# A four-layer diffusion backbone on one core: split activations stored half by half with a gap, weight slots moved by 0, 64, 320 and 384 bytes

## The reference, cut to what matters

```python
h = x * (1 + scale) + shift
x = layer_norm(alpha * x + gate * f(h))        # once with f = mixer, once with f = conv_ffn
def conv_ffn(h, w_up, conv_w, conv_b, w_down):
    u = dwconv_centred(h @ w_up, conv_w, conv_b)      # 1024 -> 2 * 2816
    gate, val = jnp.split(u, 2, axis=-1)
    return (jax.nn.silu(gate) * val) @ w_down         # 2816 -> 1024
```

## Time and profile before

| | before |
|---|---|
| median of the runs | 2409.9 us (2 runs, 2409.35 to 2410.45) |
| profiled execution, first to last instruction | 2413.2 us |
| PE busy | 2340.2 us, 97% |
| DVE, ACT, POOL busy | 70%, 47%, 14% |
| TensorE's granted clock, mean | 0.991 |
| chain that ended last, share on L1690 | 74% |

### The profile page before, as it was taken

How to read it: one execution, slowest core, us unless ns; L and a number is a source line. 1 busy time by engine, 2 the same in 40 slices (tenths; PEclk the granted TensorE clock), 3 DMA queues, 4 the chain that set the end, 5 groups by cost and what they waited for, 6 DMA issues and landing times.

```text
span 2413.2 us, 35782 instructions
## 1 busy us (share of the span) xinstructions
PE 2340.2 (97%) x13872; PEld 1903.1 (79%) x13872; DVE 1696.3 (70%) x2583; ACT 1129.2 (47%) x1948; POOL 335.6 (14%) x269
## 2 busy tenths in 40 slices
PE   6999999999999989999999999899999999989998
PEld 3765888888888559888879877788888889848998
DVE  3376689988444777999875236768999845487875
ACT  3466643442442576434324444455434325386663
POOL 0000311111110003111112003422111102002110
PEclk9999999999999999999999999999999999999999
DMA  8621645557233113555563421043555645404664
GB/s 260 204 71 39 215 142 164 166 148 208 81 97 92 30 58 100 166 157 166 162 180 86 113 70 45 2 132 114 166 163 158 192 116 125 129 13 123 187 180 132
DMA packets 449420, 310.94 MB, mean 129 GB/s; under 512 B 11922, under 2 KB 404674, under 8 KB 448996
## 3 DMA queue, kind: packets, MB, share of 16 engines
q1 hardware_dynamic: 446480, 307.09, 43.2%
q10 hardware_dynamic: 2772, 1.56, 0.2%
HBM read 307.56 MB, written 1.05 MB: 128 GB/s over the span
## 4 chain that ended last, share of the span: by engine, by line
PE 85%; DVE 6%; ACT 4%; issue 2%; DMA 2%; ACTq 0%; SPq 0%; DVEq 0%
PE bank L1690 74%; PE bank L1973 2%; DMA slab_raw<-in_mod_w 2%; PE bank L1993 1%; PE bank L2037 1%; ACT p L793 1%; DVE slab_lo L1047 1%; DVE stat L1316 1%; ACT hb L610 1%; DVE q_part L1375 1%; PE bank L1749 1%; PE bank L1768 1%; ACT slab_hi L595 1%; ACT pt L805 1%; PE bank L2165 1%
## 5 line engine op out<-in xcount | busy, mean ns | idle before, releaser
L1690 PE MATMUL bank<-h_hi,slab_hi 128*128 128x512 f32 (+1 forms) x2416 | 841.9, 348 | 4.1 <-DVE h_lo L1112 2.5
L1690 PE MATMUL bank<-h_hi,slab_lo 128*128 128x512 f32 (+1 forms) x2416 | 828.9, 343 | 0.0
L1690 PE MATMUL bank<-h_lo,slab_hi 128*128 128x512 f32 (+1 forms) x2416 | 828.9, 343 | 0.0
L1047 DVE TENSOR_TENSOR slab_lo<-slab_raw,slab_hi 128x1024 fp32r<-128x1024 f32 (+1 forms) x388 | 526.2, 1357 | 296.1 <-ACT slab_hi L595 294.8
L595 ACT ACTIVATE slab_hi<-slab_raw 128x1024 fp32r<-128x1024 f32 (+1 forms) x388 | 400.8, 1034 | 303.8 <-PE bank L1690 228.0
L1690 PEld LDWEIGHTS bank<-h_hi,slab_hi 128*128 128x128 f32 x2416 | 458.0, 190 | 85.6 <-issue 19.8
L1690 PEld LDWEIGHTS bank<-h_hi,slab_lo 128*128 128x128 f32 x2416 | 458.0, 190 | 53.8
L1690 PEld LDWEIGHTS bank<-h_lo,slab_hi 128*128 128x128 f32 x2416 | 458.3, 190 | 53.3 <-issue 0.5
L1021 ACT ACTIVATE conv<-bank,prm 128x512 f32<-128x512 f32 (+1 forms) x176 | 127.7, 725 | 446.6 <-PE bank L1690 446.6
L1072 DVE SCALAR_TENSOR_TENSOR mod_sum<-slab_raw,cond_wide,mod_sum 128x512 f32<-128x512 f32 x420 | 316.5, 812 | 0.3 <-DMA slab_raw<-in_mod_w 0.2
L1690 PE MATMUL bank<-g_hi,slab_hi 128*128 128x512 f32 (+1 forms) x788 | 272.0, 345 | 0.0
(11 more groups left out here) (248 smaller groups left out, 2658.0 us busy)
## 6 DMA issues: line engine op xcount, KB each, us to landing
slab_raw<-in_ffn_w_up SPq DMA_DIRECT2D x176, 512.0 KB, 3.9
slab_raw<-in_mod_w SPq DMA_DIRECT2D x168, 512.0 KB, 4.6
slab_raw<-in_ffn_w_down SPq DMA_DIRECT2D x64, 512.0 KB, 3.6
slab_gap<-in_mod_w SPq DMA_DIRECT2D x24, 512.0 KB, 7.6
slab_raw<-in_ffn_w_down SPq DMA_DIRECT2D x32, 384.0 KB, 3.2
slab_raw<-in_b_w_qkv SPq DMA_DIRECT2D x24, 512.0 KB, 3.8
slab_raw<-in_c_w_in SPq DMA_DIRECT2D x24, 512.0 KB, 3.8
slab_raw<-in_d_w_qkv SPq DMA_DIRECT2D x24, 512.0 KB, 3.8
```

The source lines that it names most:

```text
L1047: nc.vector.tensor_tensor(wlo[slot][:, 0:w], raw[of][:, 0:w], whi[slot][:, 0:w].bitcast(f32), ALU.subtract).then_inc(s_lo, 1)
L1690: ins = mm(out, l, r, start=first and n == 0, stop=last and n == 2, skip_group_check=parted)
```

## The change

1. `h_hi` and `h_lo` become `[P, 2, DT * CTX + H_GAP]`: first the context tokens of all 8 feature tiles (8192 bytes), then a gap of 80 float32 (320 bytes), then the latents of all 8 tiles. `g_hi` and `g_lo` become `[P, 2, FT * CTX + G_GAP]` with `G_GAP = 0`. A whole product is now one matmul with a moving access pattern of two rows of 256; a half has one row.
2. Slot s of the weights starts `SLOT_STEPS[s]` = 0, 64, 320 or 384 bytes (modulo 512) behind `h_hi`, and `whi[s]` and `wlo[s]` of a slot lie next to each other.
3. Small tensors (`coef0`, `coef1`, `small`) move into the gaps and `state[1][1]` behind `spread`; nothing else moves in time.
4. All accesses go through new views; PSUM banks and work tiles are viewed as two rows of 256 where the other operand is.

The distances, modulo 512 bytes, of moving operand less loaded weights in the same slot:

| slot | h, first half (context) | h, second half (latents) | g, either half |
|---|---|---|---|
| before, all | 0 | 0 | 64 |
| 0 | 0 | 320 | 448 |
| 1 | 448 | 256 | 384 |
| 2 | 192 | 0 | 128 |
| 3 | 128 | 448 | 64 |

A whole product of `h` has the first number while its first 256 columns move and the second after them. (For `g`: the tensors between are now 4736 + 4096 + 768 + 64 + 2048 + 1152 = 12864 = 25 x 512 + 64 bytes, behind slot 3's 384, which makes 448 behind `h_hi`.)

```diff
+SLOT_STEPS = (0, 64, 320, 384)
+H_GAP, G_GAP = 80, 0
...
-        h_hi, h_lo = place("h_hi", [P, DT, T], f32r), place("h_lo", [P, DT, T], f32r)
+        h_hi = place("h_hi", [P, 2, DT * CTX + H_GAP], f32r)
+        top[0] -= 8 * H_GAP % 512
+        h_pads = [[top[0] - 4 * H_GAP + 8 * H_GAP % 512], [top[0] + 4 * DT * CTX]]
+        h_lo = place("h_lo", [P, 2, DT * CTX + H_GAP], f32r)
+        top[0] -= 4 * H_GAP
         raw = [place(f"slab_raw{s}", [P, SLAB]) for s in range(SLOTS)]
-        whi = [place(f"slab_hi{s}", [P, SLAB], f32r) for s in range(SLOTS)]
-        wlo = [place(f"slab_lo{s}", [P, SLAB], f32r) for s in range(SLOTS)]
+        whi, wlo = [], []
+        for s in range(SLOTS):
+            top[0] += (h_at[0] + SLOT_STEPS[s] - top[0]) % 512
+            whi.append(place(f"slab_hi{s}", [P, SLAB], f32r))
+            wlo.append(place(f"slab_lo{s}", [P, SLAB], f32r))
...
-        g_hi, g_lo = place("g_hi", [P, FT, T], f32r, at=at), place("g_lo", [P, FT, T], f32r, at=at)
+        g_hi, g_lo = (place(n, [P, 2, FT * CTX + G_GAP], f32r, at=at) for n in ("g_hi", "g_lo"))
...
+        def tiles_of(x, k, c):
+            first, last = c.start // CTX, (c.stop - 1) // CTX
+            if first != last:
+                return x[:, :, CTX * k:CTX * k + CTX]
+            start = CTX * k + c.start - CTX * first
+            return x[:, first, start:start + c.stop - c.start]
+        def like(x, c):
+            return x[:, c].rearrange("p (s t) -> p s t", t=CTX) if c.stop - c.start == T else x[:, c]
...
-                nc.scalar.activation(h_hi[:, 2 * pr:2 * pr + 2, c], hb[b][:], ACT.Copy).then_inc(s_hhi, 1)
+                nc.scalar.activation(pair_of(h_hi, pr, c), hb[b][:], ACT.Copy).then_inc(s_hhi, 1)
...
-                    nc.scalar.activation(g_hi[:, j, c], g32[j % 2][:, c], ACT.Copy).then_inc(s_ghi, 1)
+                    nc.scalar.activation(tiles_of(g_hi, j, c), like(g32[j % 2], c), ACT.Copy).then_inc(s_ghi, 1)
...
-                    ins = three(out[:, c], whi[slot][:, wc], wlo[slot][:, wc], x_hi[:, k0 + k, c], x_lo[:, k0 + k, c],
+                    ins = three(like(out, c), whi[slot][:, wc], wlo[slot][:, wc], tiles_of(x_hi, k0 + k, c),
+                                tiles_of(x_lo, k0 + k, c),
                                 first and k == 0, last and k == nk - 1, parted=parted)
```

More of the change, by code:

```diff
@@ L230, in build_program @@
         modT = [place(f"modT{s}", [P, N_MOD * DT, 2]) for s in range(2)]
-        coef = [place(f"coef{s}", [P, 6, DT]) for s in range(2)]
+        coef = [place(f"coef{s}", [P, 6, DT], at=h_pads[s]) for s in range(2)]
         unit_gb = place("unit_gb", [P, 2, DT])
@@ L240, in build_program @@
         cond = cond_wide[:, cond_pad:].rearrange("p (k c) -> p k c", c=TILE)
-        small = place("small", [P, 32])
+        small = place("small", [P, 32], at=h_pads[1])
         mean_at = [top[0]]
@@ L307, in build_program @@
         decay = [place(f"decay{s}", [P, 2, 2, 2 * CH], at=at) for s in range(PART_BUFS)]
-        state = [[place(f"state{d}{s}", [P, C_HV], at=at if s < 2 else mean_at) for s in range(3)] for d in range(2)]
+        state = [[place(f"state{d}{s}", [P, C_HV], at=spread_at if (d, s) == (1, 1) else at if s < 2 else mean_at)
+                  for s in range(3)] for d in range(2)]
         z_raw = place("z_raw", [P, DT, 64], at=z_at)
@@ L496, in unit_gates, with gate_tiles @@
         def unit_gates(u):
-            return (g_ctx, g_lat)[u % 2][:, :, CH * (u // 2):CH * (u // 2) + CH]
-        def by_gate(tile_u):
-            return tile_u.rearrange("p (n k) -> p n k", n=4)
+            v = (g_ctx, g_lat)[u % 2][:, :, CH * (u // 2):CH * (u // 2) + CH]
+            return v.rearrange("p (a b) k -> p a b k", a=2)
+        def gate_tiles(rest, u):
+            v = both(g_first[rest][:]) if u == split_order[0] else tiles_of((h_hi, h_lo)[rest], u, c_all)
+            return v.rearrange("p a (b k) -> p a b k", b=2)
         def halves_of(ap, l):
@@ L821, in attention @@
                                 act.wait_ge(S["o_normed"], o + 1)
-                                nc.scalar.activation(h_hi[:, o, :], o32[:], ACT.Copy).then_inc(S["o_hi"], 1)
+                                nc.scalar.activation(tiles_of(h_hi, o, c_all), both(o32[:]), ACT.Copy).then_inc(S["o_hi"], 1)
                         continue
@@ L863, in round_gates @@
                 u = split_order[k]
-                dst = h_hi[:, u, :] if k else g_first[0][:]
-                nc.scalar.activation(by_gate(dst), unit_gates(u), ACT.Copy).then_inc(S["g_hi"], 1)
+                dst = gate_tiles(0, u)
+                nc.scalar.activation(dst, unit_gates(u), ACT.Copy).then_inc(S["g_hi"], 1)
             def gla_tables():
@@ L941, in head_hi @@
                         act.wait_ge(S["o_normed"], 2 * hd + v + 1)
-                        nc.scalar.activation(h_hi[:, 2 * hd + v, :], o_head[v][:], ACT.Copy).then_inc(S["o_hi"], 1)
+                        nc.scalar.activation(tiles_of(h_hi, 2 * hd + v, c_all), both(o_head[v][:]), ACT.Copy).then_inc(S["o_hi"], 1)
                 act.wait_ge(s_used, n_v + 8)
@@ L1580, in round_rest @@
                     dve.wait_ge(s_ghi, FT * i + 1 + j)
-                    nc.vector.tensor_tensor(g_lo[:, j, c], g32[j % 2][:, c], g_hi[:, j, c].bitcast(f32),
+                    nc.vector.tensor_tensor(tiles_of(g_lo, j, c), like(g32[j % 2], c), tiles_of(g_hi, j, c).bitcast(f32),
                                             ALU.subtract).then_inc(s_glo, 1)
@@ L1706, in project_pair @@
                         slot, wc = (n + j) % SLOTS, slice(k * P, (k + 1) * P)
-                        ins = three(outs[j][:, c], whi[slot][:, wc], wlo[slot][:, wc], h_hi[:, k, c], h_lo[:, k, c],
+                        ins = three(like(outs[j], c), whi[slot][:, wc], wlo[slot][:, wc], tiles_of(h_hi, k, c), tiles_of(h_lo, k, c),
                                     k == 0, k == DT - 1)
@@ L1836, in v_project @@
                         tc = slice(tt * P, tt * P + P)
-                        ins = three(out, whi[slot][:, wc], wlo[slot][:, wc], h_hi[:, k, tc], h_lo[:, k, tc],
+                        ins = three(out, whi[slot][:, wc], wlo[slot][:, wc], tiles_of(h_hi, k, tc), tiles_of(h_lo, k, tc),
                                     k == 0, k == DT - 1, moving_w=True)
@@ L1905, in qkv_norm_rope @@
                                 slot, wc = (n + j) % SLOTS, slice(k * P, (k + 1) * P)
-                                ins = three(bank[(fg + j) % 4][:], whi[slot][:, wc], wlo[slot][:, wc], h_hi[:, k, :],
-                                            h_lo[:, k, :], k == 0, k == DT - 1)
+                                ins = three(both(bank[(fg + j) % 4][:]), whi[slot][:, wc], wlo[slot][:, wc],
+                                            tiles_of(h_hi, k, c_all), tiles_of(h_lo, k, c_all), k == 0, k == DT - 1)
                                 if k == DT - 1:
@@ L2085, in exponents @@
                     for p in range(2):
-                        g = slice(CH * (2 * p + d), CH * (2 * p + d) + CH)
-                        for n, x in enumerate((h_hi[:, u, :], h_lo[:, u, :]) if u else (g_first[0], g_first[1])):
-                            ins = mm(out[:, 2 * CH * p:2 * CH * p + 2 * CH], x[:, g],
+                        for n in range(2):
+                            ins = mm(out[:, 2 * CH * p:2 * CH * p + 2 * CH], gate_tiles(n, u)[:, p, d, :],
                                      summed[:, d, 2 * q:2 * q + 2, :].rearrange("p l t -> p (l t)"), start=n == 0, stop=n == 1)
@@ L2099, in qkv_gla @@
                         for k in range(DT):
-                            ins = three(bank[4][0:64, :], z_hi[:, k, :], z_lo[:, k, :], h_hi[:, k, :], h_lo[:, k, :],
-                                        k == 0, k == DT - 1)
+                            ins = three(both(bank[4][0:64, :]), z_hi[:, k, :], z_lo[:, k, :], tiles_of(h_hi, k, c_all),
+                                        tiles_of(h_lo, k, c_all), k == 0, k == DT - 1)
                         ins.then_inc(S["z_full"], 1)
@@ L2122, in out_tiles @@
                     wc = slice(k * P, (k + 1) * P)
-                    ins = three(out[:], whi[n % SLOTS][:, wc], wlo[n % SLOTS][:, wc], h_hi[:, k, :], h_lo[:, k, :],
-                                k == 0, k == DT - 1)
+                    ins = three(both(out[:]), whi[n % SLOTS][:, wc], wlo[n % SLOTS][:, wc], tiles_of(h_hi, k, c_all),
+                                tiles_of(h_lo, k, c_all), k == 0, k == DT - 1)
                 if done:
```

31 lines of the change are left out of this document (19 added, 12 removed).

## The result

The changed kernel takes 2438.9 us (2 runs, 2438.25 and 2439.51) against 2409.9 before: ratio 1.0118, 95% interval 1.0089 to 1.0148. It is slower by 29 us, where 16 us less were forecast, and it lies outside the range. At 1.2% it stays within the 2% to which the prediction gave 0.82.

A forecast was written before the change was run, and what follows sets the result against it. The prediction took the kernel to be bound by the rate of split products on PE. Terms -4.9 - 11 - 1.6 + 1.4 = -16 us took the median from 2409.9 to 2394 us, range 2352 to 2432.

The forecast's parts named there:

- What bounds the kernel: PE, busy 97% of the span: the rate of split products on L1690, 1873 us, 137 us above one column per period.
- Whole products of h: 512-column products on PE: 220 ns in slot 0, 226 in the others, mean 224.5 against 226.9; 11 us saved.
- the jump at column 256: In slot 0's whole h products, the second row's 320-byte jump avoids the reads meeting again, halving the 13.6 ns loss.
- The sign that I had named for a wrong prediction: Whole products' mean pitch moving by more than 5 ns either way, which is 23 us.
- B: Rival, chance 0.20: distance 0 is good for whole products, every other worse; +20 us, 2430 us; at worst 2446.
- Halves of h: 256-column products on PE: 118.0 ns instead of 120.0 where distance is not 0; 4.9 us saved.
- Products of g: Whole ones at 227.5 ns except slot 3, 1.6 us saved; halves from 116.6 to 118, 1.4 us lost.
- Two rows, views, DMAs: Two-row moving pattern on PE, new views on ACT and DVE, unchanged DMAs and waits: 0 altogether.
- What is late next: DVE, 91 to 92% busy in the up stages, covers a 5% PE gain; takes nothing from the sum.
- A: Rival, chance 0.17: placement does not decide; every pitch stays within a nanosecond, 2410 us give or take 4.
- C: Rival, chance 0.20: unequal halves keep the two reads apart; 78 us less, 2332 us, or halfway 2365.
- The two read ports: Skill page's claim for TensorE, cited against the whole change: no distance would matter and the time would stay.

The follow-up runs named there:

- The table: Standalone kernel, 48 split products per placement: 10 distances in one row, 10 with 256 columns, 64 two-row pairs; whole products 227.0 to 233.4 ns, no pair under 227.0.
- two_rows: The changed kernel's layout in halves and its views, with gap and slot steps set to 0: 2412.3 us, ratio 0.9996 to the kernel before.
- gap_only: The changed kernel with the 320-byte gap kept and all slot steps set to 0: 2437.8 us, ratio 1.0103 to the kernel before.
- gap_256: The changed kernel with a gap of 256 bytes and slot steps 0, 256, 256, 0: 2412.6 us against 2411.5 before, ratio 1.0001.
- parts: Standalone kernel, high parts and rests of both operands placed apart, 64 combinations each for 512 and 256 columns; 512 columns ran from 226.8 to 235.5 ns.
- tail_64: The kernel before with layer 3's halves of h after its mixer stored 192 bytes lower: 2409.3 us against 2411.5, ratio 0.9986.

## Why the prediction was wrong

- *What bounds the kernel*: right. The pitch on L1690 is the time, and a change of it passes through in full: 26.6 us from the pitches, 22.9 to 29.0 in the times.
- *Whole products of h*: this step failed, in sign and size. I gave slots 1 to 3 226 ns and slot 0 220; they run at 232.6 to 233.5, so 11 us saved became 26 us lost. Two arguments were wrong. The first was that the loss arises once beside the first half, so that a whole product could be read off the half of the same first distance. But distance 0 is the worst place for 256 columns (120.0) and the best for 512 (227.0), and at 192 they lose 6.6 to 11.2 and 20.1 ns; that both lose 13.3 to 13.7 at distance 0, on which I built, is no rule. The rows said so, 226.9 to 229.1 against 120.0 to 113.2, I named it as speaking against the picture, and did not let it decide. The second was the jump at column 256, which was to keep the reads apart at the load's end. The table has all 64 pairs, and none gains. The sign that I had named for a wrong prediction came: the mean of whole products moved by 6.0 ns, over the 5. Taking a value between the bounds of 214.5 and 232.9 was the slip behind both: the three rows at full rate were 226.9, 229.1 and 232.9, the lower bound was a product at half rate, and the nearest rows spoke for B.
- *Halves of h*: right in sign, 118.5 on average over the span (118.0 taken); 4.3 us saved against 4.9.
- *Products of g*: wrong in the same way for the whole ones. Slots 0 to 2 run at 232.1 to 233.2, not 227.5: 3.8 us lost where 1.6 saved were expected. The halves were right, 1.3 us lost against 1.4.
- *Two rows, views, DMAs*: right at 0, shown by two_rows.
- *What is late next*: not tested, since PE got slower.
- *Rivals*: B happened, in the place that it named (though 256 turned out as good as 0); its price in the whole products (232.9 ns, with slot 0 spared) was right for three slots, and slot 0 was not spared. Its worst case, 2446, was nearer than its middle, 2430. I gave it 0.20, and cut the range at 2432, inside what B covers. A is refuted by gap_only against gap_256: the same instructions at other distances, 1% apart. C did not occur in any of 64 pairs.
- *The two read ports*: that loading the next weights takes no bandwidth from the running matmul (the Trainium skill, "TensorE: Matmul & The Clock Gate", Part 2) does not fit the pitch of float32r products: 227.0 to 233.4 ns with nothing changed but the place of the weights. The Trainium skill, same page, under "Back-to-back issue gap", has about 216 ns for 512 columns as the gap of single matmuls, and about 131 ns a matmul for a stream of loads and matmuls. No stream here comes near the second: with the moving operand from one address it is 216.6, with a walking one never under 226.7.

What stays open: what repeats every 256 bytes, and whether it is the meeting of the two reads at all; how a walking load can be better than a still one; on what the pitch depends where high part and rest lie apart; why one placement has two steady patterns and what selects one. A product with no load beside it was not tried, since every matmul here brings its own.

## What to carry to other kernels

Where float32r products bound a kernel, measure the pitch from the starts in the timeline and look at the start addresses of moving operand and weights modulo 256 bytes: here 512 columns want 0 (227.0 ns), and any other place costs up to 3%, while 256 columns are slowest at 0 and 96 (120.0 and 119.8) and run at 113.3 to 118.7 at 32, 64, 128 and 192. This holds where high parts and rests lie alike; any other placement has to be measured as a whole. Where rows of two forms answer a parameter in opposite ways, price each form from its own rows only, and don't carry a loss from one to the other. When the best point is a narrow one and the kernel stands on it, a change that leaves it in many directions at once is likely to lose in most of them.

## What the runs showed of the hardware that I had not expected

- The pitch of split products of 512 columns, with high parts and rests placed alike, goes by the distance of moving operand and loaded weights modulo 256 bytes: 227.0, 229.1, 232.6, 233.4 ns at 0, 64, 128, 192, and the same again at 256 to 448. At 32 and 96 it is 233.4 and 233.2.
- With the parts placed apart, distance 0 to every load does not give 227: 231.3 and 233.6 ns (parts).
- A matmul whose moving operand stands still at one address runs at 216.6 ns for 512 columns; a walking one at 226.7 or more, even beside a load of 32 columns or of one address (230.6 to 231.9). With a step of two elements the moving read takes twice the time (48 matmuls in 21.9 us, 453 ns each).
- The same code at the same distances ran at 113.3 ns in one stage and 117.7 in the next (tail_64), steadily over a thousand matmuls.
